# The FFN down projection of a decoder step by seven products of half-size blocks, with sums on GpSimd

## The reference

```python
    x = x + mix.astype(x.dtype) @ w_out
    u = rmsnorm(x, g_ffn) @ w_up
    x = x + jnp.square(jax.nn.relu(u)) @ w_down
```

## Time and profile before

| | us |
|---|---|
| three runs | 1556.29, 1560.1, 1560.49 |
| median | 1560.1 |
| span of the profiled execution | 1556.7 |
| PE busy in it | 1498.3 (96%) |
| DVE busy | 852.5 (55%) |
| ACT busy | 479.9 (31%) |
| POOL busy | 206.3 (13%) |
| phase g: PE from 809.2 to the last matmul at 1547.8 | 738.6 |
| end of the span after the start of the last matmul | 8.9 |

### The profile page before, as it was taken

The page is one execution under the profiler, slowest core; times in us unless marked ns, Lnnn a source line. Parts: engine busy times, 40 slices in busy tenths (PEclk is TensorE's granted clock), DMA queues, the critical chain, the costliest instruction groups (busy, mean ns, idle before and its releaser), DMA issues.

```text
span 1556.7 us, 27891 instructions
## 1 busy us (share of the span) xinstructions
PE 1498.3 (96%) x11634; PEld 1318.1 (85%) x11634; DVE 852.5 (55%) x1729; ACT 479.9 (31%) x943; POOL 206.3 (13%) x298
## 2 busy tenths in 40 slices
...
DMA packets 104559, 127.24 MB, mean 82 GB/s; under 512 B 26611, under 2 KB 78647, under 8 KB 103539
## 3 DMA queue, kind: packets, MB, share of 16 engines
...
...
## 4 chain that ended last, share of the span: by engine, by line
PE 89%; DVE 5%; ACT 2%; issue 2%; DMA 1%; SPq 1%; POOL 0%; DVEq 0%; ACTq 0%
PE PS L340 22%; PE PS L342 22%; PE PS L341 21%; PE PS L1644 2%; PE PS L1665 2%; PE PS L2204 2%; PE PS L2206 2%; PE PS L2205 2%; PE PS L1684 2%; PE PS L1918 2%; PE PS L350 1%; PE PS L1928 1%; PE PS L1484 1%; DVE R_att L1747 1%; DMA R_cache<-in_cache_attn_v 1%
## 5 line engine op out<-in xcount | busy, mean ns | idle before, releaser
L340 PE MATMUL PS<-x_high,R_up 128*128 128x352 f32 x768 | 249.6, 325 | 0.6 <-DVE R_upos L2496 0.6
L2506 DVE TENSOR_TENSOR R_x<-R_x,PS 128x512 f32<-128x512 f32 (+1 forms) x272 | 182.0, 671 | 123.7 <-PE PS L342 117.9
L342 PE MATMUL PS<-x_high,R_up 128*128 128x352 f32 x768 | 247.7, 322 | 0.0
L341 PE MATMUL PS<-x_low,R_up 128*128 128x352 f32 x768 | 246.8, 321 | 0.0
L2452 ACT ACTIVATE R_usq<-R_upos 128x352 f32<-128x352 f32 x96 | 47.8, 498 | 552.4 <-issue 365.1
L340 PE MATMUL PS<-R_down,R_u 128*128 128x512 f32 x512 | 202.2, 395 | 0.5 <-DVE R_u L2486 0.5
L342 PE MATMUL PS<-R_down,R_u 128*128 128x512 f32 x512 | 201.6, 394 | 0.0
L341 PE MATMUL PS<-R_down,R_u 128*128 128x512 f32 x512 | 201.1, 393 | 0.0
L2496 DVE TENSOR_SCALAR R_upos<-PS 128x352 f32<-128x352 f32 x96 | 50.3, 525 | 247.9 <-PE PS L342 242.8
L340 PEld LDWEIGHTS PS<-x_high,R_up 128*128 128x128 f32 x768 | 144.1, 188 | 7.0 <-issue 7.0
L341 PEld LDWEIGHTS PS<-x_low,R_up 128*128 128x128 f32 x768 | 144.7, 188 | 0.0
...
## 6 DMA issues: line engine op xcount, KB each, us to landing
...
```

The source lines that it names most:

```text
L340: pe.matmul(out, ll, rh, start=(k == 0), stop=False)
L341: pe.matmul(out, lh, rl_, start=False, stop=False)
L342: mm = pe.matmul(out, lh, rh, start=False, stop=(k == n - 1))
L2506: dve.tensor_tensor(part, part, PS[:, 4 + j % 4, 0:w], ALU.add).then_inc(d_taken, 1)
```

## The change

The down projection takes blocks of 512 features (`NF` = 4, 8 blocks). The block's down part splits tokens, features and output columns in halves and uses Strassen's scheme in Winograd's form: seven products of 512 tokens by 256 features by 512 columns in place of eight. Each is a `step` of PE, 24 matmuls of 512 columns, in the order P1, P2, P6, P7, P5, P3, P4. Their operands are quarters of the hidden block (`q11` to `q22`, in `R_u`) and of the weights (`w11` to `w22`, in `R_raw`) or sums of quarters: four sums of weights and three of hidden values on POOL (`T_1` to `T_4`, `S_1`, `S_3`, `S_4`), one (`s2`) on DVE. All are float32 in SBUF, 128 partitions by 1024 values, most in place of a quarter that is not needed again.

The split now happens per operand: ACT copies the high part of each of the 14 operands of a block (`left_high_part`, `right_high_part`), DVE subtracts the low part of the seven left ones and of the last five right ones, POOL of the first two right ones. There are two buffers per side (`ua`, `wb`), so the parts for a step are written once the step two before has ended (`operand_free`). POOL also takes over the low parts of the `w_up` chunks, which are now one feature tile each, in a ring of three. P1, P6 and P7 share PSUM banks and accumulate on them, as do P5 and P3; a step that accumulates waits until DVE has added the state before it (`d_taken`). The sample tokens' product (now 16 matmuls) stands ahead of P1.

At the start of phase g SP loads two `w_up` chunks and four rows of `w_down` ahead of `g_sample`; the wide `g_final` row comes at the end, when the up pieces are done. In the last block tiles 0 to 3 are complete with P3, tiles 4 to 7 with P4; `final` of the sample tile and of tiles 0 to 2 stands between the adds of P4, the rest behind them.

```diff
-FB = 256
-NF = FB // P
-NBLK = DFF // FB
-wup = i_["w_up"][0].rearrange("(c k p) n -> c p k n", k=4, p=P)
+NF = 4
+NUP = DFF // P
+NBLK = NUP // NF
+wup = i_["w_up"][0].rearrange("(k p) n -> p k n", p=P)
...
+for F in range(NUP):
+    CHUNKS.append((at(R_up[F % 3], 0), at(R_up[F % 3], 1024), wup[:, :, F * P:(F + 1) * P],
+                   at(R_first if F < 2 else R_stage, F % 2 * 1024)))
...
+q11, q12, q21, q22 = (quarter(U, j, i, HT) for i in range(2) for j in range(2))
+w11, w12, w21, w22 = (quarter(raw, j, n, HN) for j in range(2) for n in range(2))
+s2, t2 = view(R_s2, 0, f=2, t=HT), view(R_stage, 1024, f=2, t=HT)
+ua = [[view(r, 1024 * z, f=2, t=HT) for z in range(2)] for r in R_ua]
+wb = [[view(r, 1024 * z, f=2, t=HN) for z in range(2)] for r in R_wb]
...
+P1, P2, P6, P7, P5, P3, P4 = STEPS = range(7)
+LEFT = {P1: q11, P2: q12, P6: s2, P7: q21, P5: q11, P3: q12, P4: q22}
+RIGHT = {P1: w11, P2: w21, P6: t2, P7: w12, P5: w11, P3: w22, P4: w21}
+OPENS = (P1, P2, P5, P4)
+SECOND_BANKS = (P2, P5, P3)
+ADDED_TO = {P1: [(0, 0)], P2: [(0, 0)], P6: [(0, 1)], P7: [(1, 0), (1, 1)], P5: [(1, 1)], P3: [(0, 1)], P4: [(1, 0)]}
+ND = 1 + 7 * 4
+POOL_LOWS = (P1, P2)
+S_3, T_1, T_2, T_3, T_4, S_1, S_4 = range(7)
...
+LAST_TILES = [NCH, 0, 1, 2, 3, 4, 5, 6, 7]
+def product_index(b, k, p):
+    return ND * b + 1 + 4 * k + p
+def product_bank(k, p):
+    return p if k in SECOND_BANKS else 4 + p
...
+def operand_free(eng, b, k):
+    G = 7 * b + k
+    if G >= 2:
+        pb, pk = divmod(G - 2, 7)
+        eng.wait_ge(d_psum, product_index(pb, pk, 3) + 1)
...
     sp.wait_ge(norm_split, 2 * NTILE)
-    sp.dma_start(grow, i_["g_final"].rearrange("(o d) -> o d", o=1).to_broadcast([P, D])).then_inc(x1_in, 16)
+    load_chunk(sp, KD + 2)
+    load_chunk(sp, KD + 3)
+    raw_rows(0, 0)
+    raw_rows(0, 1)
     for j in range(4):
         sp.dma_start(g_sample[32 * j:32 * j + 32],
                      i_["g_final"][256 * j:256 * j + 256].rearrange("(o d) -> o d", o=1).to_broadcast([NS, 256])).then_inc(x1_in, 16)
-    load_chunks(sp, DOWN_CHUNKS[0], len(CHUNKS))
+    for b in range(NBLK - 1):
+        for F in (NF * b + 4, NF * b + 5, NF * b + 6):
+            sp.wait_ge(chunk_split, NW + KD + F - 1)
+            load_chunk(sp, KD + F)
+        sp.wait_ge(dve_split, dve_count(b, P6, "right"))
...
+        sp.wait_ge(dve_split, dve_count(b, P5, "right"))
+        raw_rows(b + 1, 0)
+        sp.wait_ge(dve_split, dve_count(b, P4, "right"))
+        raw_rows(b + 1, 1)
...
+    sp.wait_ge(u_psum, NU * NBLK)
+    sp.dma_start(R_gain, i_["g_final"].rearrange("(o d) -> o d", o=1).to_broadcast([P, D])).then_inc(x1_in, 16)
...
+    def step(b, k):
+        pe.wait_ge(dve_split, dve_count(b, k, "right" if k == P6 else "left"))
...
+        (uh, ul), (wh, wl) = ua[(7 * b + k) % 2], wb[(7 * b + k) % 2]
+        for p in range(4):
...
+            if k in (P6, P7, P5, P3, P4):
+                pe.wait_ge(d_taken, product_index(b, {P6: P1, P7: P6, P5: P2, P3: P5, P4: P7}[k], p) + 1)
+            out, ts = PS[:, product_bank(k, p), :], slice(p * P, (p + 1) * P)
+            for f in range(2):
+                pe.matmul(out, ul[:, f, ts], wh[:, f, :], start=(f == 0 and k in OPENS), stop=False, skip_group_check=True)
+                pe.matmul(out, uh[:, f, ts], wl[:, f, :], start=False, stop=False, skip_group_check=True)
+                mm = pe.matmul(out, uh[:, f, ts], wh[:, f, :], start=False, stop=(f == 1), skip_group_check=True)
+            mm.then_inc(d_psum, 1)
...
+    def left_high_part(b, k):
+        operand_free(act, b, k)
+        if k == P6:
+            act.wait_ge(s2_ready, b + 1)
+        if k in (P7, P5, P3):
+            act.wait_ge(pool_sums, sums_count(b, {P7: S_3, P5: S_1, P3: S_4}[k]))
+        act.activation(ua[(7 * b + k) % 2][0], LEFT[k], ACT.Copy).then_inc(operand_high, 1)
+    def right_high_part(b, k):
+        operand_free(act, b, k)
+        if k in (P1, P2):
+            raw_loaded(act, b, k)
+        if k in (P6, P7, P5, P4):
+            act.wait_ge(pool_sums, sums_count(b, {P6: T_2, P7: T_3, P5: T_1, P4: T_4}[k]))
+        act.activation(wb[(7 * b + k) % 2][0], RIGHT[k], ACT.Copy).then_inc(operand_high, 1)
...
+        left_high_part(b, P2)
+        left_high_part(b, P6)
+        right_high_part(b, P6)
+        for k in (P7, P5, P3, P4):
+            right_high_part(b, k)
+            left_high_part(b, k)
+            if k == P5 and not last:
+                up_high(NF * b + 6)
...
+def phase_g_gps(pool):
...
+    for b in range(NBLK):
+        last = b == NBLK - 1
+        up_low(NF * b + 3 if b else 2)
+        if not b:
+            up_low(3)
+        right_low_part(b, P1)
+        right_low_part(b, P2)
+        pool.wait_ge(u_squared, NU * b + 6)
+        pool.tensor_tensor(q21, q11, q21, ALU.subtract).then_inc(pool_sums, 1)
+        if not last:
+            up_low(NF * b + 4)
+            up_low(NF * b + 5)
+        pool.wait_ge(d_psum, ND * b + 1)
+        pool.wait_ge(right_split, 2 * b + POOL_LOWS.index(P2) + 1)
+        pool.tensor_tensor(w11, w12, w11, ALU.subtract).then_inc(pool_sums, 1)
+        pool.wait_ge(pool_sums, sums_count(b, T_1))
+        pool.tensor_tensor(t2, w22, w11, ALU.subtract).then_inc(pool_sums, 1)
+        pool.tensor_tensor(w12, w22, w12, ALU.subtract).then_inc(pool_sums, 1)
+        pool.wait_ge(pool_sums, sums_count(b, T_2))
+        pool.tensor_tensor(w21, w21, t2, ALU.subtract).then_inc(pool_sums, 1)
+        pool.wait_ge(s2_ready, b + 1)
+        pool.wait_ge(dve_split, dve_count(b, P2, "left"))
+        pool.tensor_tensor(q11, q11, s2, ALU.add).then_inc(pool_sums, 1)
+        pool.tensor_tensor(q12, q12, s2, ALU.subtract).then_inc(pool_sums, 1)
+        if not last:
+            up_low(NF * b + 6)
...
+    def added(b, k, p):
+        j = product_index(b, k, p)
+        dve.wait_ge(d_psum, j + 1)
+        before = {P1: (b - 1, P2), P2: (b, P1), P6: (b - 1, P3), P7: (b - 1, P4), P5: (b, P7), P3: (b, P6), P4: (b, P7)}[k]
+        if before[0] >= 0:
+            dve.wait_ge(d_taken, product_index(before[0], before[1], p) + 1)
+        for i, n in ADDED_TO[k]:
+            part = x1[:, 4 * i + p, n * HN:(n + 1) * HN]
+            ins = dve.tensor_tensor(part, part, PS[:, product_bank(k, p), :], ALU.add)
+        ins.then_inc(d_taken, 1)
...
-    dve.wait_ge(x1_in, 16 * 18)
+    dve.wait_ge(x1_in, 16 * 17)
...
+        dve.wait_ge(u_squared, NU * (b + 1))
+        dve.wait_ge(pool_sums, sums_count(b, S_3))
+        dve.tensor_tensor(s2, q22, q21, ALU.subtract).then_inc(s2_ready, 1)
+        left_low_part(b, P2)
+        dve.wait_ge(d_psum, ND * b + 1)
+        dve.tensor_tensor(x1s, x1s, PS[:, 7, 0:256], ALU.add).then_inc(d_taken, 1)
+        for p in range(4):
+            added(b, P1, p)
+        dve.wait_ge(s2_ready, b + 1)
+        left_low_part(b, P6)
+        added(b, P2, 0)
+        right_low_part(b, P6)
+        for p in range(1, 4):
+            added(b, P2, p)
+        added(b, P6, 0)
...
+        right_low_part(b, P3)
+        left_low_part(b, P3)
+        for p in range(4):
+            added(b, P5, p)
+        added(b, P3, 0)
+        right_low_part(b, P4)
+        left_low_part(b, P4)
+        for p in range(1, 4):
+            added(b, P3, p)
+        for p in range(4):
+            added(b, P4, p)
+            if last:
+                if p == 0:
+                    dve.wait_ge(x1_in, 16 * 18)
+                final(LAST_TILES[p])
+    for i in LAST_TILES[4:]:
+        final(i)```

**DVE, down part of a block.** Before, the adds to the residual (`R_x`) with two low parts of the next block's `w_up` between them, and then the next block's first up pieces:

```order
L2506 TENSOR_TENSOR R_x<-R_x,PS 128x512 [waits d_psum] x4
L2095 TENSOR_TENSOR R_up<-R_stage,R_up 128x1024 [waits chunk_high]
L2506 TENSOR_TENSOR R_x<-R_x,PS 128x512 [waits d_psum] x6
L2095 TENSOR_TENSOR R_up<-R_stage,R_up 128x1024 [waits chunk_high]
L2506 TENSOR_TENSOR R_x<-R_x,PS 128x512 [waits d_psum] x6
L2506 TENSOR_TENSOR R_x<-R_x,PS 128x256 [waits d_psum]
```

More of the change, by code:

```diff
@@ L1835, in phase_e_sync @@
             sp.wait_ge(ov_psum, 1)
-            load_chunks(sp, 0, KD)
+            for m in range(KD):
+                load_chunk(sp, m)
         def load_caches(sp, items):
@@ L2234, in phase_f2_sync @@
             sp.wait_ge(op_psum, 10)
[L2235 removed]
+            for F in range(2):
+                load_chunk(sp, KD + F)
             sp.dma_start(token_sum, const("c_token_sum")).then_inc(x1_in, 16)
@@ new lines, in program @@
+        ND = 1 + 7 * 4
+        POOL_LOWS = (P1, P2)
+        S_3, T_1, T_2, T_3, T_4, S_1, S_4 = range(7)
+        HIGH_ORDER = [(P1, "right"), (P2, "right"), (P1, "left"), (P2, "left"), (P6, "left"), (P6, "right")] + [
+            (k, side) for k in (P7, P5, P3, P4) for side in ("right", "left")]
+        DVE_ORDER = [(P1, "left"), (P2, "left"), (P6, "left"), (P6, "right"), (P7, "right"), (P7, "left"), (P5, "right"),
```

(38 more changed lines are left out.)

265 lines of the change are left out of this document (126 added, 139 removed).

## The result

The changed kernel takes 1564.1 us (median of 18 runs, 1558.9 to 1572.0) against 1558.6 (18 runs, 1554.9 to 1563.7) for the kernel before: ratio 1.0035, 95% interval 1.0023 to 1.0046. It is slower, as forecast, but by 5.5 us and not by 10. The profiled execution's span is 1562.7 us, 6.0 more than before.

A forecast was written before the change was run, and what follows sets the result against it. PE's own work, 96% busy, bounds the kernel. Start 8.3 us, pieces, down part, seven periods of 92.6 us and last block put PE's end at 1549.8; plus 17.2 gives 1567.0, moved onto the median 1570 us; 8-in-10 range 1549 to 1580.

The forecast's parts named there:

- without collision: DVE's low parts and POOL's sums run side by side, 36 us less, 1534 us; chance 0.12.
- with half the waits: DVE waits for half a POOL instruction on average, 2.4 us a block go, 1550 us; chance 0.14.
- with POOL keeping the port: A waiting DVE isn't let in during POOL's chain; P6's left part waits about 8 us, 1610 us; chance 0.04.
- the four steps named: P6, P7, P5 and P3 in each block start 1.8, 1.1, 1.0 and 0.7 us late, waiting for operands.
- the other two pages of the Trainium skill: Pages on DVE performance modes: GpSimd collides in two-port mode, which tensor_tensor lacks, so low parts would pass POOL untouched.
- one down matmul: Down steps on PE: 0.232 us per matmul of 512 columns, 1344 of them in place of 1536.
- sample product: Sample tokens' product at each block's head: 8 x 2.36 us in place of 16 x 1.36.
- late starts and all else in a block: Waits ahead of four steps plus 4 x 0.2 us of restart: 5.4 us a block.
- start, up to the first sample product: Start of phase g: small loads queue behind six 512 KB loads, costing 8.3 us with stall and clock.
- end behind the last matmul: DVE's remaining adds and finals end 14.0 us behind the last step, then 3.2 us: 17.2 us.
- the stall: Start of phase g: PE, two up pieces done at 816.8, stands 6.6 us until DVE's ReLU at 823.4.
- The clock's lower level: After PE's stop at the start of phase g, 1.2 GHz for 3.5 us, half added: 1.7 us.

The follow-up runs named there:

- one_input: Changed kernel with DVE's four low parts of P6 and P7 replaced by one-SBUF-input instructions writing zeros; 1552.9 us, ratio 0.9943 to the kernel before.

## What the prediction had right, and the step that failed

**Right: direction and mechanism.** The forecast's rivals without collision (1534), with half the waits (1550) and with POOL keeping the port (1610) all failed; DVE and POOL take turns by whole instructions, as the earlier trace rows had shown, and the four steps named were the four that wait. Of the pages weighed there, "SBUF — State Buffer" of the Trainium skill (Who interferes with whom), by which DVE's second pair of SBUF ports is POOL's own and held exclusively, fits both the two-input instructions (1.21 us alone, 2.45 to 3.35 beside POOL) and the one-input ones of `one_input`; for the former, the prediction's reading of the other two pages of the Trainium skill, that only two-port modes collide, is refuted by the rows above.

**The sum, term by term** (profiled execution against profiled execution; forecast 1567.0, measured 1562.7):

| term | forecast | measured | difference |
|---|---|---|---|
| one down matmul | 0.232 us | 0.2267 | 1344 x 0.0052 = -7.0 |
| sample product | 2.36 | 1.86 | 8 x 0.5 = -4.0 |
| late starts and all else in a block | 5.4 | 5.9 | +4.1 |
| start, up to the first sample product | 855.7 | 858.2 | +2.5 |
| end behind the last matmul | 17.2 | 17.3 | +0.1 |

(The third row's difference is what the measured 687.2 us from the first sample product to the last matmul leave.) Two prices were too high, by 11 us together, and the waits and the start too low, by 6.6; that the errors partly cancel is luck.

**The step that failed** is the first price: "Eleven steps from 985.28 to 987.83 give 0.232 us per matmul of 512 columns". The number is right for the kernel before; the error was to carry it to steps whose loaded operand is another tensor, where a matmul takes 0.2267 us: 7.0 us too much. The trace of the kernel before has no 512-column product at the other price (those of phase f1 load from rows of 1056 columns too, and stand 0.232 us apart), so it took a run to tell.

**The sample product** is the second term: I doubled 1.00 us and added 0.36, and 32 matmuls take 1.86. The 0.36 was a misreading: that row is the first matmul of the next up piece. Counted between starts, the 16 matmuls took 1.00 us (PE's timeline of the kernel before; the last row ends the six up pieces):

```profile
988.14 1.07 PE L350 MATMUL PS<-R_raw,R_ur 128*32 128x256 f32 x16
989.15 0.43 PE L340 MATMUL PS<-x_high,R_up 128*128 128x352 f32 x1
...
1012.32 0.39 PE L340 MATMUL PS<-R_down,R_u 128*128 128x512 f32 x1
```

The same rows make an up piece 23.17/6 = 3.86 us and not 3.82. That 3.82 came out in the changed kernel (45.90/12 = 3.825) is luck; no run here shows why a piece got shorter.

**Late starts**: 1.8, 1.1, 1.0, 0.7 forecast; 1.75, 1.26, 1.07, 0.97 measured. P3's is off most: DVE's work from P5's operands to P3's took the 6.6 us of the layout (1070.1 to 1076.7), but P5 itself took 5.58 us and not the 5.8 laid out, so that PE stood longer.

**The start**: I took the small loads to land at 823 and the stall at 6.6; they were issued from 816.4, DVE started at 824.67 and PE stood 8.43. The clock's lower level lasted 4.2 us into the work, for which I had put 1.7 us of cost; it is 2.1.

**Against the median**: the forecast was set on 1560.1, the median of three runs; 18 runs give 1558.6, which is 1.5 of the 5.9 us by which 1570 was too high.
